# Hybrid decoder step on one core: plain weight-sum copies issued from ScalarE's queue, three clearings moved to GpSimd, one output-weight piece loaded at another place

## The reference, cut to what matters

```
h    = rms_norm(x, ln_w)
proj = h @ w_in                      # 1024 x 8720: q, k, v, gates of both branches
A:   three groups of dilated windowed attention (128/1, 512/4, 2048/16), mixed by their log-sums
B:   gated linear attention with a 64 x 128 state per head, in chunks of 64
mix: sigmoid(ma) * (A * silu(az)) @ w_attn_out + sigmoid(mb) * (norm(B) * silu(gz)) @ w_gla_out
y    = rms_norm(x + mix @ w_out) ; also the key/value windows and the GLA states
```

## Time and profile before

| what | value |
|---|---|
| median of three runs (lowest, highest) | 2366.73 us (2366.71, 2373.11) |
| the profiled execution's own time | 2376.85 us |
| its span, first to last instruction | 2375.1 us |
| mean granted TensorE clock | 0.984 |
| PE busy | 2276.9 us (96%) |
| DVE busy | 1696.5 us (71%) |
| ACT busy | 806.0 us (34%) |
| POOL busy | 300.9 us (13%) |
| DMA queue q1 (SP) | 358.77 MB, 44.5% of 16 engines |
| DMA queue q0 (POOL) | 166.36 MB, 27.1% |
| DMA queue q10 (ACT) | 25.96 MB, 2.9% |

### The profile page before, as it was taken

How to read it: one execution, slowest core, us unless ns; L and a number is a source line. 1 busy time by engine, 2 the same in 40 slices (tenths; PEclk the granted TensorE clock), 3 DMA queues, 4 the chain that set the end, 5 groups by cost and what they waited for, 6 DMA issues and landing times. The chain is left out here.

```text
span 2375.1 us, 36222 instructions
## 1 busy us (share of the span) xinstructions
PE 2276.9 (96%) x12996; PEld 1835.6 (77%) x12996; DVE 1696.5 (71%) x3309; ACT 806.0 (34%) x1705; POOL 300.9 (13%) x491
## 2 busy tenths in 40 slices
PE   7999999889999999999999999889999898999998
PEld 5788778767788888888878887668788646888887
DVE  6756567757785688888877876887888758556663
ACT  5332221112224432211212232767767524122121
POOL 1000012212110011222212220112111000000000
PEclk8999999999999999999999999999999999999999
DMA  8999999999997567888787888767465497434431
GB/s 264 239 283 324 284 280 281 240 243 280 291 270 228 189 178 252 256 270 262 248 245 226 278 270 305 258 209 229 161 200 182 135 325 289 180 126 160 169 143 65
DMA packets 271184, 553.40 MB, mean 233 GB/s; under 512 B 33392, under 2 KB 60480, under 8 KB 268896
## 3 DMA queue, kind: packets, MB, share of 16 engines
q1 hardware_dynamic: 200688, 358.77, 44.5%
q0 software_dynamic: 58000, 166.36, 27.1%
q10 hardware_dynamic: 12320, 25.96, 2.9%
HBM read 442.60 MB, written 191.50 MB: 267 GB/s over the span
## 5 line engine op out<-in xcount | busy, mean ns | idle before, releaser
L1675 PE MATMUL b_acc<-b_whi,a_hi 128*128 128x512 f32 x1792 | 707.6, 395 | 20.2 <-DVE b_wlo L1338 13.6
L1677 PE MATMUL b_acc<-b_whi,a_lo 128*128 128x512 f32 x1792 | 701.7, 392 | 0.0
L1676 PE MATMUL b_acc<-b_wlo,a_hi 128*128 128x512 f32 x1792 | 701.4, 391 | 0.0
L1675 PEld LDWEIGHTS b_acc<-b_whi,a_hi 128*128 128x128 f32 x1792 | 339.0, 189 | 93.6 <-issue 16.0
L1088 ACT CAST b_whi<-b_w 128x2048 fp32r<-128x2048 f32 (+1 forms) x127 | 228.7, 1802 | 531.1 <-PE b_acc L1677 349.7
L1677 PEld LDWEIGHTS b_acc<-b_whi,a_lo 128*128 128x128 f32 x1792 | 338.3, 189 | 71.3
L1676 PEld LDWEIGHTS b_acc<-b_wlo,a_hi 128*128 128x128 f32 x1792 | 339.1, 189 | 68.4
L1338 DVE TENSOR_TENSOR b_wlo<-b_w,b_whi 128x2048 fp32r<-128x2048 f32 (+1 forms) x127 | 273.1, 2151 | 88.0 <-ACT b_whi L1088 88.0
L1132 ACT ACTIVATE c_sm<-c_sm,c_ends 128x256 f32<-128x256 f32 (+1 forms) x384 | 172.5, 454 | 8.5 <-DVE c_ends L1486 8.3
L1486 DVE CUSTOM_DVE_ANT_0 c_sm<-c_p_s,c_mask 128x256 f32<-128x256 f32 (+1 forms) x384 | 120.3, 360 | 36.7 <-PE c_p_s L1764 34.8
L991 POOL DMA_DIRECT2D a_x<-tm x188 | 107.4, 580 | 249.8 <-DVE sT L1452 174.7
(11 more groups left out here) (374 smaller groups left out, 3486.8 us busy)
## 6 DMA issues: line engine op xcount, KB each, us to landing
b_w<-t SPq DMA_DIRECT2D x64, 1024.0 KB, 8.4
t<-in_w_in POOLq DMA_DIRECT2D x48, 1024.0 KB, 11.5
b_w<-in_w_in SPq DMA_DIRECT2D x47, 1024.0 KB, 8.1
a_x<-tm POOLq DMA_DIRECT2D x167, 256.0 KB, 7.1
tm<-b_st SPq DMA_DIRECT2D x128, 256.0 KB, 7.5
b_ck<-in_cache_kv_w POOLq DMA_DIRECT2D x96, 256.0 KB, 5.2
c_qk<-tm SPq DMA_DIRECT2D x96, 256.0 KB, 3.5
t<-t POOLq DMA_DIRECT2D x16, 1024.0 KB, 11.8
```

The lines of the kernel that those rows point to most:

```text
L1675: nc.tensor.matmul(out, stat_hi, mov_hi, start=first, stop=False)
L1676: nc.tensor.matmul(out, stat_hi, mov_lo, start=False, stop=False)
L1677: return nc.tensor.matmul(out, stat_lo, mov_hi, start=False, stop=last)
```

## The change

Three edits.

1. *Weight sums.* The set of turn 0 stays as it was (`first_sums`). In each of the eight other sets the four copying DMAs go to ACT's queue (`copy_weights`, semaphore `t_copied`): b22 to T3 and b11 to T2 at step 0, b21 to T4 and b11 to T1 at step 1, in ACT's program three slots behind the slot of the step. POOL keeps the four adding ones: T3 at step 2, T2 and T1 at step 3, T4 at step 4.
2. *Clearings.* `e_pn` and the two `e_pm` are cleared by POOL, ahead of its loads of `g_state`, after the same wait for the end of the recurrence; DVE clears only the piece of `gss`. The two waits for `cleared` now want all four.
3. *Output weights.* Piece 1 of `w_attn_out` is loaded where the load of `e_vc_weights` and `e_vn_b` stands, at the end of the projection. The small constants of the recurrence count on `const_in` in place of a semaphore of their own.

```diff
-T_DMAS = 8
+T_DMAS, T_ADDS = 8, 4
...
+            if n == 0:
+                return 16 * (T_DMAS // 2 if form in (T2, T3) else T_DMAS)
+            return 16 * (T_DMAS + T_ADDS * (n - 1) + (T_ADDS if form == T4 else T_ADDS - 1))
...
+                def weight_sums(turn, step):
+                    b12 = w_block(turn, 0, 1)
+                    t1, t2, t3, t4 = [t_part(turn.n, form, w_cols(turn, 0)[1]) for form in (T1, T2, T3, T4)]
+                    done, copied = t_due(turn, T4) - 16 * T_ADDS, 16 * T_ADDS * sums_no[turn.n]
+                    if step == 2:
+                        pool.wait_ge(t_in, done)
+                        pool.wait_ge(t_copied, copied)
+                        pool.dma_start(t3, b12, accum_op=ALU.add, max_dma_last_dim=2048).then_inc(t_in, 16)
+                    elif step == 3:
+                        pool.wait_ge(t_in, done + 16)
+                        pool.dma_start(t2, t3, accum_op=ALU.add, max_dma_last_dim=2048).then_inc(t_in, 16)
+                        pool.dma_start(t1, b12, accum_op=ALU.add, max_dma_last_dim=2048).then_inc(t_in, 16)
+                    elif step == 4:
+                        pool.wait_ge(t_in, done + 48)
+                        pool.dma_start(t4, t2, accum_op=ALU.add, max_dma_last_dim=2048).then_inc(t_in, 16)
...
+                def copy_weights(turn, step):
+                    width = w_cols(turn, 0)[1]
+                    if step == 0 and sums_no[turn.n] > 1:
+                        act.wait_ge(t_in, t_due(turn, T4) - 32 * T_ADDS + 16)
+                    for form, row, n in (((T3, 1, 1), (T2, 0, 0)) if step == 0 else ((T4, 1, 0), (T1, 0, 0))):
+                        act.dma_start(t_part(turn.n, form, width), w_block(turn, row, n)).then_inc(t_copied, 16)
...
+                    for n, step in sums_at.get(s - 3, ()):
+                        if step < 2:
+                            copy_weights(turns[n], step)
...
+                load_wb(1)
...
+        over.recurrence_over(pool)
+        nc.gpsimd.memset(pn[:, :, :, :], 0.0).then_inc(cleared, 1)
+        nc.gpsimd.memset(pm1[:, :, :, :], 0.0).then_inc(cleared, 1)
+        nc.gpsimd.memset(pm2[:, :, :, :], 0.0).then_inc(cleared, 1)
...
-            act.wait_ge(cleared, 3)
+            act.wait_ge(cleared, 4)
...
-            V.memset(pn[:, :, :, :], 0.0).then_inc(cleared, 1)
-            V.memset(pm1[:, :, :, :], 0.0).then_inc(cleared, 1)
-            V.memset(pm2[:, :, :, :], 0.0).then_inc(cleared, 1)
```

24 lines of the change are left out of this document (14 added, 10 removed).

## The result

The changed kernel is slower: median 2385.39 us (four runs, 2384.57 to 2389.39) against 2366.72 us (four runs, 2365.48 to 2373.11) of the kernel before. The ratio is 1.0061, 95% interval 1.0041 to 1.0082; the medians lie 18.7 us apart. Forecast was 2351 us, with 2332 to 2369 as the range. The time lies outside it, near the 2379 us of the rival *the loads lose*, to which I had given 0.11. The profiled execution of the changed kernel took 2389.39 us, with a span of 2387.6 us.

The account below looks back on a forecast made before the run. PE was busy 2276.9 of 2375.1 us, so only its waits and lost clock could be won. Terms 7.5 + 0 + 3 + 3.8 + 1.3 = 15.6 us, taken from 2366.73, gave 2351 us; range 2332 to 2369.

Parts of the forecast that it names:

- the loads lose: Rival, chance 0.11: copies on ACT's queue meet SP's weight loads, four gaps of 7 us, so slower, 2379 us.
- the gap at 449 us: PE waits 7.04 us for `b_wlo` in the projection; 2 us put to the late query, 5 to the load.
- Edit 1 (a): Weight sums: waits for copies leave POOL's program, queries go out up to 6.5 us earlier; 7.5 us together with (b).
- rival on late sums: Rival that ACT reaches its copy issues late and POOL waits at step 2; counted within the loads lose, no own chance.
- Edit 1 (b): Weight sums: copies cost 3.0 us per MB, go out some 20 us earlier; load near 438 us lands after 8, not 11.5.
- Edit 1 (c): Turn 5's gaps, 10.8 us in all: no net change, 0 us, bounds +8 and -10.8.
- Edit 1 (d): The other projection gaps, 11.6 us over the other turns: a quarter won, 3 us, bounds 0 and 11.6.
- Edit 1 (e): ACT gets 32 copy issues, each under a microsecond beside PE work; bound 2.7 us each, as on SP.
- Edit 2, 3.8 us: Clearings moved to POOL, between recurrence and sample: DVE starts the masks earlier, 3.8 us won, bounds 2.6 and 5.
- Edit 3, 1.3 us: Output weights: piece 1 loaded early, so the last piece comes one issue earlier; 1.3 us won, bounds 0 and 2.8.
- The sums aren't moved in time: The rival on late sums: in-order ACT issues copies late behind casts that wait for PE; given no chance of its own.
- The rule on queues: Skill's rule that DMA engines alternate between queues: a third queue would leave SP's weight loads a third of turns, not half.

Follow-up runs that it names:

- e11: Kernel before with edits 2 and 3, old sums, the sample's early queries begun at turn 5 instead of turn 3: ratio 1.0088 to the kernel before.
- e12: Changed kernel with the sample's early queries begun at turn 5 instead of turn 3: ratio 1.0169 to the kernel before.
- e17: Kernel before with edit 3 alone (piece 1 of the output weights loaded elsewhere): ratio 1.0000 to the kernel before.
- e2: Kernel before with edits 2 and 3 alone, weight sums all made by POOL as before: ratio 0.9990 to the kernel before.
- e18: The same file as e2, edits 2 and 3 without edit 1, run again: ratio 0.9988 to the kernel before.
- e6: Changed kernel with the sets of turns 5 and 7 made as before, in five steps on POOL: ratio 1.0016 to the kernel before.
- e14: Changed kernel, a semaphore for each pair of copies, first pair at its step's slot, second pair waiting for PE: ratio 1.0014 to the kernel before.
- e4: Changed kernel with the copies issued on POOL's own queue at steps 0 and 1: ratio 1.0018 to the kernel before.
- e5: Changed kernel with the copies three slots earlier in ACT's program: ratio 1.0040 to the kernel before.

## Why the prediction was wrong, step by step

- **What bounds the kernel, and the gap at 449 us: right.** The chain POOL, query, DVE, `b_wlo` is what the gap is made of; without queries there it is gone (e11, e12). I had split it as 2 us for the query and 5 for the load. No run shows the split: without queries there is no gap, but the 1 MB load landed sooner too, after 5.5 us (e11) and not 11.5, so the queries make themselves and the load late.
- **Edit 1 (a), waits on POOL: wrong, and the step that failed.** I said that the waits for copies leave POOL's program and the queries go out up to 6.5 us earlier. One wait for copies stays, for all four, and in turn 4 it is 17.8 us. In the rival on late sums I had written that "between the copies' slot and step 2 lie four to seven slots". That counts from the first pair (seven slots in most sets, three in turn 5's). The second pair stands at step 1 plus three slots, two slots ahead of step 2 in most sets; in turn 5's set, with three slots to a step, that is the slot of step 2 itself. The numbers stood in the code; I took the first pair's distance for both.
- **Edit 1 (b), time of issue: wrong.** I had the copies out "some 20 us earlier, ahead of 415 us" and one add in flight at 438 us. The first pair went out at 410 us, 16 us later than POOL's, of which 8.4 us are PE's own delay by then and the rest the three slots. The second went out 2 us behind it, since ACT's program has one small copy between them and its slot isn't PE's. At 438 to 454 us three adds were to come. The load took 12.6 us, not 8, the query 16.7. In place of 7.5 us won, the block behind the gap starts 18.4 us later than before: 1.8 lost ahead of turn 3's mark, 6.6 by the set of turn 4 and 10.0 in the gap.
- **Edit 1 (b), the price of a copy: right.** DMA queue of ACT, changed kernel, 60 to 720 us (packets, MB, share of engines):

```profile
q10 hardware_dynamic: 16896, 31.46, 14.4%
```

  31.46 MB on ACT's queue took 14.4% of the engines from 60 to 720 us: 0.144 x 660 / 31.46 = 3.0 us of all engines for a MB, as on POOL's.
- **Edit 1 (c), turn 5: the size was off within its bounds.** Its gaps in the changed kernel have one of 9.84 us, where the longest was 4.23; but PE's busy time from 480 to 540 us is 50.0 us, as before (49.2), though the two windows no longer hold the same blocks.
- **Edit 1 (d), the other gaps: wrong sign.** 3 us were to go. They grew: 6.61 us near 642 us where 1.53 and 2.21 stood; there too POOL waits for four copies (14.0 us at 606 us). And the 2.3 and 2.2 us at the start of turn 4 are new; with the lower clock behind them they cost 6.6 us.
- **Edit 1 (e), ACT: right.** An issue costs about 0.6 us (1.18 for two, 2.62 at the most in turn 4), and the cast behind the second pair in turn 4 waited 0.85 us for it. ACT isn't held up by the copies; the copies are held up by ACT's place in time.
- **Edit 2, 3.8 us: right.** From the last score product to the first `e_p_o` product (timeline of PE, before, then changed):

```profile
1876.44 1.16 PE L1764 MATMUL c_p_s<-c_kT,c_qT 64*128 64x128 f32 x16
...
1897.19 2.07 PE L2353 MATMUL e_p_o<-e_vn_a,e_pnT 48*128 48x512 f32 x2
```

```profile
1891.92 1.16 PE L1800 MATMUL c_p_s<-c_kT,c_qT 64*128 64x128 f32 x16
...
1909.19 2.07 PE L2395 MATMUL e_p_o<-e_vn_a,e_pnT 48*128 48x512 f32 x2
```

  20.75 us became 17.27: 3.5 won. PE's 2.62 us wait for `c_pT` is gone. POOL cleared beside DVE (timeline of POOL, then DVE, changed kernel):

```profile
1894.62 2.02 POOL L2348 MEMSET e_pm<- 128x2304 f32 x1
...
1895.16 0.69 DVE L1532 COPY c_pT<-c_p_t 128x512 f32<-128x512 f32 x1
```

  This copy, out of PSUM, ran inside the clearing (which lasts until 1896.6 us) in its usual 0.69 us, as the nearest row had before. The Trainium skill, "SBUF — State Buffer", section "Who interferes with whom", has GpSimd and VectorE share a pair of ports that one of them holds, but exempts a VectorE instruction with at most one SBUF input outside the two-port modes. The trace agrees with that. I had read it as if it held for every copy; the 1.8 us that I took from it does not follow from it for a copy without an SBUF input.
- **Edit 3, 1.3 us: the gain came and was given back.** Timeline of PE at the first products of the output, changed kernel, where the earlier trace rows had 4.00 us:

```profile
1978.90 0.50 PE L2485 MATMUL f_p_b<-w_wb_hi,f_bT_hi 128*128 128x512 f32 x1 [2.29 <-DVE f_bT_lo L3031]
...
1987.62 0.55 PE L2485 MATMUL f_p_b<-w_wb_hi,f_bT_hi 128*128 128x512 f32 x1 [2.94 <-DVE w_wb_lo L2915]
```

  From the first `e_p_o` to the first `f_p_b` product it is 69.7 us where it was 70.8, so 1.1 us won. The next block then waits 2.94 us where it waited 1.50: its weights are loaded when the first are cast, and come no sooner. From the first `f_p_b` to the last it is 399.5 us where it was 397.8. Net about nothing, as e17 measured. I had not asked what is late next.
- **The rivals.** *The loads lose* had the sign and 2379 us, and its price was near by luck: four gaps of 7 us. Its mechanism was loads that share the engines, and its deciding point a 1 MB load that lands after 11 us. That one load did (12.6 us), but from 60 to 720 us the median landing of SP's 1 MB loads is what it was (11.5 us for pieces before and after, 10.1 and 10.2 us for sums); what stopped PE longest was the query behind POOL's waits. *The sums aren't moved in time* was the right mechanism, and I had dismissed it with the wrong count of slots, as a part of the first. It should have had a chance and a price of its own.
- **The rule on queues.** The traces show three queues with work in turn 4 and longer landings there: the query 16.7 us where it took 12.8, with the copies on POOL 9.9. They also show six sets of copies on the third queue, and all eight when issued earlier, at 0.27 and 0.25% over e2 and e18 (e6, e14), with the copies back on POOL's queue at 0.28% over e2 (e4): no more for the third queue. The Trainium skill, "DMA: Bandwidth & Descriptors", section "Queues, rings and completion order", says that each engine takes turns between queues with work. By it alone a third queue would have cost the weight loads in every turn. Their median landing over the stage didn't change, and from 100 to 300 us PE waited 3.2 us for `b_wlo` where it had waited 3.4. So it doesn't carry the loss, though it may be part of the longer landings in turn 4, which no run here takes apart from the bytes in flight.

## What to carry to other kernels

When work is moved to another engine's queue, ask where that engine's program stands in time, not in slots: count for each consumer the distance to the *last* thing it waits for, and place the issue in terms of the engine that paces the program. A wait for a whole group, in an in-order queue that also feeds a latency-bound consumer, costs that consumer the landing of everything in the group; count the parts apart. And a stage that is DMA-full need not cost PE anything (e11 and e12, turn 4): look for the short transfer with a reader waiting, since here it was the one that came late. Compare more than one mark when two kernels are set side by side, since a kernel can lose in one turn what it wins in the next (e6).

## What the runs showed that I had not expected

- In a full stage a 256 KB query took longer the more was in flight with it: 5 to 13 us beside 1 MB of adds or none, 16.7 us in turn 4 of the changed kernel, with 2 MB of copies ahead of it and 2 MB more 4.6 us behind, and 21.8 us in e5, where 4 MB of copies went out at the same time. With the copies on POOL's own queue (e4, 454 to 459 us) it took 9.6 to 17.8 us.
- Four copies of 512 KB issued together on an otherwise idle queue had a median landing of 14.8 us, and the last was seen 20 us after its issue; POOL's two at a time had landed within 11 us.
- Kernels with identical instructions in a stage run it in 513 to 524 us, from one build and execution to the next, and the kernel before ranges from 2361 to 2383 us over all its runs. Effects of under 0.3% can't be read from a few runs of this kernel: with ten to twelve the intervals of e2 and e18 are still 0.15 to 0.18% to either side. Traces tell smaller ones, where the stretch has no DMA-bound waits in it.
